# Down projection weights in single row blocks of 512 KB, and their highs ahead of M6's on ScalarE

## The reference, cut to what matters

```python
def conv_ffn(xn, buf, w_up, w_conv, b_conv, w_down):
    u, gt = jnp.split(xn @ w_up, 2, axis=-1)
    up = jnp.concatenate([buf.astype(u.dtype), u], axis=1)
    conv = b_conv
    for j in range(CONV_W):
        conv = conv + w_conv[j] * up[:, j:j + t]
    y = (jax.nn.silu(conv) * gt) @ w_down
```

## Time and profile before

| | us |
|---|---|
| median of 3 runs | 1691.96 (1686.0 to 1702.23) |
| the profiled execution | 1694.95 |
| its span, first to last instruction | 1693.2 |
| TensorE busy | 1591.4 (94%), 14375 matmuls |
| VectorE busy | 1038.8 (61%) |
| ScalarE busy | 724.9 (43%) |
| GpSimd busy | 306.5 (18%) |
| mean granted TensorE clock | 0.984 |
| up loads on SP | 180 of 256 KB, median 3.5 us to landing |
| sums on GpSimd | 144 of 256 KB, median 4.7 us to landing |
| down loads on SP | 20, median 7.7 us to landing (16 of 1 MB, 4 of 512 KB) |

### The profile page before, as it was taken

One profiled execution on the slowest core, in us unless ns is written; L12 is line 12 of the kernel. 1 busy time (PEld: TensorE's weight loads), 2 busy tenths in 40 slices (PEclk: granted clock), 3 DMA queues, 4 the chain that ended last, 5 costly groups with the idle time before them and its releaser, 6 DMA issues.

```text
span 1693.2 us, 37537 instructions
## 1 busy us (share of the span) xinstructions
PE 1591.4 (94%) x14375; PEld 1432.9 (85%) x14375; DVE 1038.8 (61%) x2518; ACT 724.9 (43%) x1585; POOL 306.5 (18%) x434
## 2 busy tenths in 40 slices
PE   6999999988999999999989999998799999999997
PEld 5899975557999999999989997645689999999997
DVE  3544446657487867758564354575656877768765
ACT  3322237634243734536342213664333444635434
POOL 1011104422102212212001101252210121212111
PEclk9999999999999999999999999999999999999999
DMA  9435297369516958766133536634845486858632
GB/s 344 136 91 186 67 366 251 118 198 180 190 60 144 215 146 181 174 158 142 54 103 92 185 116 237 224 91 151 165 78 168 96 212 148 193 153 177 168 76 65
DMA packets 234898, 266.76 MB, mean 158 GB/s; under 512 B 16074, under 2 KB 176266, under 8 KB 234268
## 3 DMA queue, kind: packets, MB, share of 16 engines
q1 hardware_dynamic: 209088, 210.90, 40.9%
q0 software_dynamic: 25632, 53.47, 16.6%
HBM read 218.21 MB, written 16.68 MB: 139 GB/s over the span
## 4 chain that ended last, share of the span: by engine, by line
PE 66%; DMA 14%; DVE 8%; ACT 4%; issue 4%; DVEq 1%; SPq 1%; POOL 1%; ACTq 1%; POOLq 0%
PE ps L1745 13%; PE ps L1120 13%; DMA slab<-slab 11%; PE ps L1609 8%; PE ps L1550 5%; PE ps L963 3%; PE ps L1598 2%; PE ps L1259 2%; PE ps L1244 2%; PE ps L1171 2%; DMA slab<-in_w_out 2%; PE ps L1104 2%; PE ps L1582 1%; PE ps L1115 1%; PE ps L1114 1%
## 5 line engine op out<-in xcount | busy, mean ns | idle before, releaser
L3439 POOL DMA_DIRECT2D slab<-slab x144 | 125.2, 904 | 586.1 <-DMA slab<-in_w_up 154.4
L1120 PE MATMUL ps<-slab_r,work_r 128*128 128x256 f32 x960 | 205.6, 282 | 0.0
L1120 PEld LDWEIGHTS ps<-slab_r,work_r 128*128 128x128 f32 x960 | 157.8, 188 | 2.7 <-issue 2.5
L1745 PE MATMUL ps<-side_r,big_r 128*128 128x272 f32 x672 | 140.6, 290 | 5.6 <-DVE xT L3027 2.9
L1745 PE MATMUL ps<-side_r,slab_r 128*128 128x272 f32 x672 | 139.0, 288 | 0.0
L1745 PE MATMUL ps<-big_r 128*128 128x272 f32 x672 | 138.6, 288 | 0.0
L1609 PE MATMUL ps<-big_r,slab_r 128*128 128x272 f32 x432 | 101.5, 296 | 16.0 <-ACT xnT L2230 9.4
L1745 PEld LDWEIGHTS ps<-side_r,big_r 128*128 128x128 f32 x672 | 105.4, 188 | 8.3 <-DVE xT L3027 3.8
L2461 DVE TENSOR_TENSOR slab_r<-slab,big_r 128x1024 fp32r<-128x1024 f32 (+1 forms) x68 | 90.4, 1348 | 25.6 <-ACT big_r L2196 16.3
L1745 PEld LDWEIGHTS ps<-big_r 128*128 128x128 f32 x672 | 105.6, 189 | 0.0
L1609 PE MATMUL ps<-work_r,more_weights_r 128*128 128x272 f32 x432 | 104.6, 295 | 0.6 <-ACT xnT L2230 0.3
(11 more groups left out here) (556 smaller groups left out, 4499.5 us busy)
## 6 DMA issues: line engine op xcount, KB each, us to landing
slab<-in_w_up SPq DMA_DIRECT2D x180, 256.0 KB, 3.5
slab<-in_w_mod SPq DMA_DIRECT2D x22, 2048.0 KB, 10.9
slab<-slab POOLq DMA_DIRECT2D x144, 256.0 KB, 4.7
slab<-in_w_in SPq DMA_DIRECT2D x20, 1024.0 KB, 5.7
slab<-in_w_down SPq DMA_DIRECT2D x20, 1024.0 KB, 7.7
slab<-in_cache_cmp_kv SPq DMA_DIRECT2D x128, 128.0 KB, 2.0
slab<-in_cache_sel_kv SPq DMA_DIRECT2D x96, 128.0 KB, 2.0
big<-in_cache_win_kv SPq DMA_DIRECT2D x16, 512.0 KB, 7.7
```

The lines of the kernel that those rows point to most:

```text
L1120: ins = mm(ps[n % 4][:, 0:cw], x, fr(wt[:, k, :]), start=k == 0 and m == 0, stop=k == KC - 1 and m == 2)
L1745: ins = mm(ps[bank + b][:, 0:HALF], wt, fr(x[:, k, HALF * b:HALF * b + HALF]), start=k == 0 and n == 0, stop=k == n_k - 1 and n == 2)
L3439: pool.dma_start(block_of(kind, c), src, accum_op=ALU.add).then_inc(sums_in[kind], 16)
```

## The change

`load_down` no longer issues the group as two transfers of 1 MB. It issues single row blocks of 512 KB on a semaphore of their own, `down_in`, and each block but the first of a group waits on SP for the landing of the block ahead of it. Row blocks 0 and 1 go where the group went before; block 2 goes behind the up loads of the loop pass c % 4 == 1, block 3 behind those of c % 4 == 2. The first group of a layer is loaded as four blocks in a row, the last as two. `split_down` on ScalarE waits for its own row block. On ScalarE the down highs of a round now stand behind the high of M7(c+1) and ahead of the high of M6(c+1). VectorE's and TensorE's order is unchanged.

```diff
--- before.py
+++ after.py
@@ -438,6 +438,7 @@
                 dmas[s] += PARTS[name] * n[s]
         for s in (0, 2):
             dmas[s] += {0: 1, 2: 2}[s] * (FC - CL)
+        dmas[1] -= PARTS["ffn"] * 6
         slab_in = [ctx.enter_context(nc.semaphore(f"slab{s}_loaded")) for s in range(NSLAB)]
         slab_out = [ctx.enter_context(nc.semaphore(f"slab{s}_used")) for s in range(NSLAB)]
 
@@ -638,6 +639,12 @@
             n = LOWS[kind, c]
             return b_lo.sem, b_lo.at(n + 1 + (4 if n >= 2 else 0), L)
 
+        down_in = ctx.enter_context(nc.semaphore("down_row_blocks_loaded"))
+
+        def down_loaded(j, k, L):
+
+            return down_in, 16 * (L * (4 * NG + 2) + 4 * j + k + 1)
+
         g1_in, third_in = [ctx.enter_context(nc.semaphore(n)) for n in ("gate_first_blocks_loaded", "sum_3_first_terms_loaded")]
         sums_in = {kind: ctx.enter_context(nc.semaphore(f"sum_{i}_added")) for i, kind in ((1, "M5"), (2, "M6"), (3, "M7"), (4, "M3"))}
 
@@ -809,10 +816,6 @@
                     dst = dst.rearrange("p (k h n) -> p k h n", k=8, h=2)
                     return [(dst[:, :, h, :], wup[L, :, :, h, q]) for h in range(2)]
 
-                def down_copies(row, n):
-                    dst = slab[1][:, 0:2 * n * D].rearrange("p (k n) -> p k n", n=D)
-                    return [(dst[:, n * i:n * i + n, :], wdn[L, :, row(n * i), :]) for i in range(2)]
-
                 def load_block(dst, h, k, c, sem):
 
                     sp.dma_start(dst.rearrange("p (k n) -> p k n", k=4),
@@ -851,14 +854,19 @@
                         sp.wait_ge(third_in, each(c - 1, L))
                     load_block(block_of("M7", c), 0, 0, c, third_in)
 
-                def load_down(j):
-
-                    n = 2 if j < NG else 1
-                    load("ffn", 1, down_copies(lambda k: slice(4 * j + k, 4 * j + k + n), n), j)
+                def load_down(j, ks):
+
+                    if 0 in ks:
+                        load("ffn", 1, [], j)
+                    for k in ks:
+                        if 4 * j + k < FC:
+                            if k:
+                                sp.wait_ge(*down_loaded(j, k - 1, L))
+                            sp.dma_start(slab[1][:, D * k:D * k + D], wdn[L, :, 4 * j + k, :]).then_inc(down_in, 16)
 
                 load("ffn", 2, up_copies(0, slice(0, 256)))
                 load("ffn", 0, up_copies(1, slice(256, 512)))
-                load_down(0)
+                load_down(0, range(4))
                 sp.wait_ge(g_acc.sem, g_acc.at(2, L))
                 sp.wait_ge(w_hi.sem, w_hi.at(3, L))
                 load_u(CL)
@@ -875,7 +883,7 @@
                 load_g1(CL + 2)
                 load_third(CL + 2)
                 load_u(CL + 2)
-                load_down(1)
+                load_down(1, (0, 1))
                 for c in range(CL, FC - 1):
                     if c + 3 < FC:
                         load_g1(c + 3)
@@ -883,7 +891,9 @@
                         load_g2(c + 3)
                         load_u(c + 3)
                     if c % 4 == 0 and c > CL:
-                        load_down(c // 4)
+                        load_down(c // 4, (0, 1))
+                    elif c % 4 in (1, 2):
+                        load_down(c // 4, (c % 4 + 1,))
 
             for n, (t, hf, _) in enumerate(FINAL):
                 if n % 2:
@@ -2192,7 +2202,8 @@
                     act.wait_ge(u_h.sem, u_h.at(cd + 1, L))
                     A_(fr(hiH[:, q, :]), hid[:, q, :], ACT.Copy).then_inc(h_hi.sem, 1)
 
-                def split_down(part, n_k):
+                def split_down(part, n_k, j):
+                    act.wait_ge(*down_loaded(j, part, L))
                     A_(fr(hiD[:, n_k * part:n_k * part + n_k, :]),
                        slab[1][:, n_k * D * part:n_k * D * (part + 1)].rearrange("p (k n) -> p k n", k=n_k), ACT.Copy
                        ).then_inc(d_hi.sem, 1)
@@ -2262,10 +2273,8 @@
                     if q == 3:
                         history_in(CL)
                     split_h(q, q)
-                    if q == 1:
-                        act.wait_ge(slab_in[1], slab_loads("ffn", 1, L))
                     for k in ((), (0, 1), (2, 3), ())[q]:
-                        split_down(k, 1)
+                        split_down(k, 1, 0)
                 product1_out(CL)
                 act.wait_ge(g_acc.sem, g_acc.at(CL, L))
                 act.wait_ge(t_sum.sem, t_sum.at(4, L))
@@ -2300,9 +2309,8 @@
                     if q != 1:
                         high("M3", c)
                     if not more_up:
-                        act.wait_ge(slab_in[1], slab_loads("ffn", 16, L))
                         for part in range(2):
-                            split_down(part, 1)
+                            split_down(part, 1, NG)
                     product5_out(c)
                     if more_up:
                         high("M2", c + 1)
@@ -2313,12 +2321,10 @@
                     first_tap(c)
                     if more_up:
                         high("M7", c + 1)
+                    for part in ((), (0, 1), (2,), (3,))[q] if g < NG else ():
+                        split_down(part, 1, g)
+                    if more_up:
                         high("M6", c + 1)
-                    if g < NG:
-                        if q == 1:
-                            act.wait_ge(slab_in[1], slab_loads("ffn", 1, L, g))
-                        for part in ((), (0, 1), (2,), (3,))[q]:
-                            split_down(part, 1)
                     silu(1, c)
                     if q == 0:
                         high("M3", c + 1)
```

## The result

The changed kernel takes **1732.7 us** (median of 6 runs, 1726.0 to 1738.7) against 1690.4 (1686.0 to 1702.2) for the one before: a ratio of 1.0233, with 95% between 1.0199 and 1.0266 (here and below the ratio is an estimate of its own; the quotient of the two medians is 1.0250). It is slower by 2.3%. The forecast was 1702 with a range of 1679 to 1725; the time is where the second rival, "late by much, and the clock falls", had put it (1731). The profiled executions stand 39.5 us apart in span (1732.7 against 1693.2), and all numbers on single rounds are from these two.

What follows compares the result with a forecast made beforehand. TensorE was taken as the bound (busy 1591.4 of 1693.2 us), so only its gaps in the rounds of blocks 5 to 21 could change. Terms -8.1 - 0.9 + 16.1 + 2.9 + 0.7 = +10.7 us gave 1702, range 1679 to 1725.

Steps and rivals of the forecast that it cites:

- late by much, and the clock falls: Rival: at L = 6.5 TensorE stands 2.9 us in eight rounds and its clock drops; +39 us, 1731; chance 0.28.
- Blocks 2, in rounds 6, 10, 14, 18: Block 2, issued behind its pass's last up piece, lands after ScalarE wants it, delaying TensorE's M6 in eight rounds: +16.1 us.
- L: Time from issue to landing of a single down block: taken as 5.3 us for blocks 2, 4.8 for blocks 3.
- the restart: Extra cost of each TensorE gap beyond its own length, 0.36 us, read from round 12 of layer 1.
- round 6, downs first: ScalarE starts the down highs while waiting in round 5, so TensorE's gaps in round 6 shrink: -8.1 us.
- VectorE's 0.15 us, seen in rounds 10, 14, 18: In rounds 9, 13, 17 VectorE no longer waits 0.15 us for the down high, six times: -0.9 us.
- blocks 3, rounds 8, 12, 16, 20: Block 3, issued in rounds 7, 11, 15, 19, lands late: 12.1 us in place of 9.2 lost today, +2.9 us.
- last pair, round 21: Block 1 goes out only when block 0 has landed, delaying its high and the copy M3 awaits: +0.7 us, two layers.
- L - 3.65: TensorE's standing time for a late block 2: L + 4.35 - 8.0 us, with 8.0 from issue to M6's need.
- A wait that goes unseen: Rival: sums of M7 and M5, delayed by new traffic, move TensorE's gaps while down blocks are in time; 1692; chance 0.08.

Runs made afterwards that it cites:

- half-size kernel: Changed kernel, but in groups 2 to 4 only 256 KB of blocks 2 and 3 stay late, the rest goes with blocks 0 and 1: 1715.4 us, ratio 1.0138.
- the order alone: Kernel before with only ScalarE's order changed, down highs ahead of M6's high, down weights still two 1 MB transfers: 1691.7 us, ratio 0.9998.
- the loads alone: Changed kernel's single row block loads, but with ScalarE's old order: 1736.7 us, ratio 1.0263 to the kernel before.

## Why the prediction was wrong

It failed in the step *Blocks 2, in rounds 6, 10, 14, 18*: "Block 2 goes out a little later and I take L = 5.3: 1.65 us, and 0.36 for the restart." By step, of the two profiled executions:

| step | forecast, us | measured, us |
|---|---|---|
| round 6, downs first | -8.1 | -9.5 |
| VectorE's 0.15 us, seen in rounds 10, 14, 18 | -0.9 | -1.5 |
| blocks 2, rounds 7, 11, 15, 19 | +16.1 | **+44.9** |
| blocks 3, rounds 8, 12, 16, 20 | +2.9 | +5.9 |
| last pair, round 21 | +0.7 | +0.9 |
| round 5 | 0 | -0.4 |
| sum | +10.7 | +40.3 (spans: +39.5) |

**The mechanism was right; the size of L was not.** ScalarE stands for a down transfer, VectorE passes it on, TensorE stands before M6, in the eight rounds named; where ScalarE asks later, most of it goes from there. The formula too: L - 3.65 with the measured mean L of the eight blocks, 7.41 us (6.67 to 8.52), gives 3.76, and the gaps of 2.96 to 4.77 us have a mean of 3.61.

**L.** 7.41 in place of 5.3 is 8 x 2.11 = 16.9 us. The value was taken from the up piece ahead of it in a kernel in which the block itself did not exist. The bounds were from the same kernel, so even the upper one (6.5) lay below the smallest measured (6.67). The block makes its own surroundings: 512 KB more in flight, with sums and pieces at 7 us around it. The half-size kernel shows that bytes count here, but weakly. By the Trainium skill (DMA: Bandwidth & Descriptors, Anatomy of one DMA), whose fit of about 2.0 us plus bytes over 436 GB/s is for transfers that GpSimd issues, an estimate for 512 KB is 3.2 us; the lone one, issued by SP, agreed, the eight in the rounds took 2.1 to 2.7 times that.

**The price of a gap.** The 44.9 us are 28.9 of gaps and 16.0 of what follows them, 2.0 for each gap and not 0.36. The 0.36 was read behind a gap of 0.24 us. Behind the gap of 3.92 the window above has 0.57. That is another 13 us: 16.1 + 16.9 + 13 = 46, about the 44.9. For the gap that the forecast had, 1.65 us, 0.36 would have been right: round 20 of layer 1 has a gap of 1.64 now and is 1.99 too long. So the dearer gap follows from L. The second rival had both parts (it took 2.9 + 1.5 for each); the error was to set the up piece's ordinary 5.4 us above it. The row that spoke for it was there: 5.67 too much with a gap of 2.72. That the rival's time, 1731, is so near is partly luck: its blocks 2 are 10 us too cheap (35 against 44.9), its blocks 3 6 us too dear (12 against 5.9).

**Blocks 3** came near, +2.9 against +5.9, by two errors that cancel. Their L was taken as 4.8 and measured 6.76 in the mean; by the forecast's own formula that would have been 8 x 3.47 - 9.2 = +18.6. But the time from issue to need was 9.6 us in the mean (9.1 to 10.7) and not 8.0: for round 12 of layer 1 it is 660.30 + 6.03 - 656.87 = 9.46. The forecast took 0.5 off the 8.5 of before, and 1 us came on top of it instead: from block 2's place to block 3's SP took 5.0 us longer than before (14.8 against 9.8), while TensorE's round, with the gap and the lower clock behind it, was 5.7 longer.

**Round 6** came out near the forecast (M6's gaps are 0.28 us where about 1 was forecast), but its reason was half of it. Of 10.8 us too much in two layers the order alone leaves 3.6, the loads alone 2.6, both 1.3; the prediction held the smaller transfers to be worth nothing there.

**Late or traffic?** Both, and not additive. Issued nine us earlier, with no wait left on the block, the loss is 20.5 us in place of 42; asked for later, 29; extra bytes at this place without any wait cost 12, almost none of it in rounds 7, 11, 15 and 19. How the 42 us split exactly can't be read from these runs: each move of the transfer changes the traffic as well, and each move of the high changes VectorE's order. The rival *A wait that goes unseen* described the traffic part in kind (late sums; it named M7's and M5's, the gaps that came are ahead of M3), as an addition and not in place of the lateness.

## What to carry to other kernels

When a transfer is moved into a busy stretch, don't take its landing time from what is there without it: put the moved bytes in, and price the range up to where every transfer in flight is slower. An engine that takes its work in order turns one late transfer into a delay of all that stands behind it; ask first how much time lies between issue and need, and whether it covers the worst landing and not the median. Gaps of TensorE of 3.6 us in the mean cost 5.6 here, while one of 0.24 cost 0.60: price a gap from rows of its own size, and from several, since gaps of 2.0 to 3.3 us here came with the clock staying up as well as falling. And if taking away one wait brings nothing, look for the chain that is only just in time behind it, here the sums.

## What the runs showed of the hardware

- A 512 KB transfer landed in 3.2 us alone and in 6.7 to 8.5 us in rounds with a DMA share of 0.80 to 0.93. The mean share did not tell this: it was 0.95 in the same round before, with 256 KB pieces at 5.4 us.
- 272 KB that nobody reads, 16 times, cost 12 us (0.8% of the time), though they are 4.5 MB of 271.
- TensorE's granted clock fell in all eight rounds with gaps of 2.96 to 4.77 us, to 0.50 or 0.57 over 4 us in the three looked at, and the gaps cost 2.0 us each on top in the mean; windows with gaps of 1.7 us and less (the order-alone kernel's rounds 6, 7 and 8) stayed at 1.00. Between 2.0 and 3.3 us both happened: 1.00 with a gap of 2.25 (changed kernel, round 8 of layer 1) and of 3.26 (half blocks late, round 7), but 0.88 with one of 1.97 (blocks nine us earlier, round 11).
